# Two transformer blocks with grouped experts: slot table loaded by ScalarE, rows of the first expert stage gathered by one-hot products, and another hand-over between the blocks

## The reference, cut to what matters

```python
def hier_moe(x2d, w_grp, b_grp, w_exp, b_exp, w_gate, w_up, w_down):
    ...                       # combine[t, e]: two weights per token
    for e in range(N_EXPERTS):
        h = jax.nn.silu(x2d @ w_gate[e]) * (x2d @ w_up[e])
        y = y + combine[:, e:e + 1] * (h @ w_down[e])
    return y
# first_block:  h = h + mix @ w_out;  h = h + moe(rmsnorm(h, norm_ffn_g));  return rmsnorm(h, final_norm_g)
# second_block: the same with rms_norm, starting from the first block's output x:
#   u = rms_norm(x, attn_norm) @ w_in;  h = x + mix @ w_out_2;  h = h + moe(rms_norm(h, ffn_norm_2)); return rms_norm(h, final_norm_2)
```

## Time and profile before

| | us |
|---|---|
| median of 3 runs | 1642.69 (1637.81 to 1642.77) |
| profiled execution, its own time | 1649.94 |
| its span | 1648.2 |
| around the span | 1.7 |
| PE busy | 1389.2 (84%) |
| DVE busy | 428.0 (26%) |
| ACT busy | 363.0 (22%) |
| POOL busy | 188.7 (11%) |
| mean granted TensorE clock | 0.919 |
| DMA traffic | 287.90 MB |

### The profile page before, as it was taken

The page is one execution under the profiler, slowest core; times in us unless marked ns, Lnnn a source line. Parts: engine busy times, 40 slices in busy tenths (PEclk is TensorE's granted clock), DMA queues, the critical chain, the costliest instruction groups (busy, mean ns, idle before and its releaser), DMA issues. The chain is left out here.

```text
span 1648.2 us, 22613 instructions
## 1 busy us (share of the span) xinstructions
PE 1389.2 (84%) x9850; PEld 696.6 (42%) x9850; DVE 428.0 (26%) x797; ACT 363.0 (22%) x617; POOL 188.7 (11%) x259
## 2 busy tenths in 40 slices
PE   5999989877897688876679999568789799999995
PEld 3434444577555233322334444367445533333332
DVE  2233315432324001101520100493522400000015
ACT  2023016443122011111231100332433111111112
POOL 5000002254001110110000000141000110000000
PEclk8989999999998798999879999886899799999998
DMA  5251100200144699999613210000224479998973
GB/s 192 97 215 51 51 0 0 104 4 4 57 179 179 241 410 417 416 414 411 228 51 124 80 52 0 1 1 1 103 76 160 176 290 365 350 344 338 347 324 132
DMA packets 77418, 287.90 MB, mean 175 GB/s; under 512 B 17057, under 2 KB 18424, under 8 KB 65026
## 3 DMA queue, kind: packets, MB, share of 16 engines
q1 hardware_dynamic: 67456, 265.33, 41.7%
q0 software_dynamic: 7680, 14.72, 2.6%
q10 hardware_dynamic: 2178, 6.34, 1.0%
HBM read 267.50 MB, written 29.84 MB: 180 GB/s over the span
## 5 line engine op out<-in xcount | busy, mean ns | idle before, releaser
L347 PE MATMUL banks<-mixT,ring 128*128 128x512 f32 x672 | 295.4, 602 | 0.8 <-DVE mixT L2400 0.8
L347 PEld LDWEIGHTS banks<-mixT,ring 128*128 128x128 f32 x672 | 130.2, 194 | 165.6 <-issue 164.4
L2144 PE MATMUL banks<-arena_moe,mixT 128*32 128x512 f32 x768 | 174.6, 601 | 0.0
L2144 PE MATMUL banks<-ring,mixT 128*32 128x512 f32 x768 | 118.0, 621 | 18.8 <-DMA arena_moe<-in_w_up 15.5
L1446 PE MATMUL banks<-ring,mixT 128*128 128x512 f32 x256 | 116.0, 609 | 8.2 <-PEq L51 8.2
L1891 PE MATMUL banks<-arena_moe,mixT 128*64 128x512 f32 x256 | 69.5, 703 | 34.1 <-DMA arena_moe<-in_exp_w_up 34.1
L344 PE MATMUL banks<-ring,mixT 128*128 128x512 f32 x192 | 82.9, 593 | 0.0
L2144 PEld LDWEIGHTS banks<-ring,mixT 128*32 128x32 f32 x768 | 37.9, 114 | 95.9 <-issue 95.9
L1446 PEld LDWEIGHTS banks<-ring,mixT 128*128 128x128 f32 x256 | 48.9, 196 | 65.6 <-issue 65.6
L1891 PE MATMUL banks<-ring,mixT 128*64 128x512 f32 x256 | 60.0, 623 | 10.9 <-DMA ring<-in_exp_w_up 7.7
L1740 DVE TENSOR_TENSOR mixT<-banks,params 128x512 f32<-128x512 f32 (+1 forms) x64 | 38.8, 623 | 111.6 <-PE banks L1731 100.6
(11 more groups left out here) (421 smaller groups left out, 1996.4 us busy)
## 6 DMA issues: line engine op xcount, KB each, us to landing
ring<-in_w_in SPq DMA_DIRECT2D x18, 1024.0 KB, 8.4
arena_moe<-in_exp_w_gate SPq DMA_DIRECT2D x16, 1024.0 KB, 13.0
arena_moe<-in_exp_w_up SPq DMA_DIRECT2D x16, 1024.0 KB, 17.9
arena_moe<-in_exp_w_down SPq DMA_DIRECT2D x16, 1024.0 KB, 22.7
ring<-in_exp_w_gate SPq DMA_DIRECT2D x16, 1024.0 KB, 14.3
ring<-in_exp_w_up SPq DMA_DIRECT2D x16, 1024.0 KB, 18.9
ring<-in_exp_w_down SPq DMA_DIRECT2D x16, 1024.0 KB, 22.4
arena_moe<-in_w_gate SPq DMA_DIRECT2D x8, 2048.0 KB, 11.0
```

The costliest lines, as they stand in the source:

```text
L347: last = pe.matmul(bank[:], w[:, c, i * P:(i + 1) * P], m.mixT[:, c, :], start=(c == 0), stop=(c == DC - 1))
L2144: last = pe.matmul(hb[u][T * i:T * (i + 1), :], z.xe[:, j, at:at + T], both[:, :, j, half * 256:half * 256 + 256], start=(j == 0), stop=(j ...
```

## The change

It does the following.

1. `load_slots` for the main table moves from SP to ScalarE's program in both blocks: after silu 1 of body 0, before hidden_taken 0. ScalarE no longer waits for the slots before body 0, but before output 0 of body 0.
2. Block 1: all bodies get their rows by one-hot products. VectorE writes G for body i+2 behind the rows of body i+1; TensorE runs 2 x 32 matmuls in place of 2 x 8 transposes; the 14 fetches by GpSimd go. Block 2: body 1 alone gets its rows that way; bodies 2 to 7 fetch as before, the fetch for body 2 being issued first.
3. `between_programs`: the scaling `store` and its write by ScalarE go; SP writes the gained rows (hg) to HBM, between the second and the third weight item of the projection. Block 2's residual is scaled when it is added (`scalar_tensor_tensor` with a kept factor in place of `tensor_tensor`). `taken(0)` to `taken(2)` move in between the statistics of later tiles, and the second square writes to another scratch.
4. Last body of block 1: early(0) and early(1) come before the `y_low_dve`, early(2) and early(3) after them.
5. Start: the two norm gains of the expert blocks are no longer loaded as rows by ScalarE and turned, but loaded turned by SP, element by element (2 x 1024 elements of 4 bytes), behind the small loads.

```diff
@@ load_slots: sp.dma_start becomes engine.dma_start; out_programs: add(i, n)
-            dve.tensor_tensor(h, h, m.banks[k % 3][:], ALU.add)
+                dve.scalar_tensor_tensor(h, h, residual_scale(i), m.banks[k % 3][:], ALU.mult, ALU.add)
@@ phase_project1, sync
+            for name, c in TURNED.items():
+                sp.dma_start(m.params[:, c:c + DC], io[name].rearrange("l (c p) -> p (l c)", p=P),
+                             allow_slow_non_contiguous=True).then_inc(ph.sem("turned_gains"), 16)
@@ gather_pe(pe, ph, z, pair, half, taken): 32 matmuls per half
+    for a in range(2):
+        if taken is not None:
+            pe.wait_ge(ph.sem("gathered_taken"), taken + a + 1)
+        for b in range(2):
+            j = 4 * half + 2 * a + b
             for t in range(NT):
                 for part in (z.x_hi, z.x_lo):
...
@@ narrow_programs, sync
-        sp.wait_ge(out.sem("tabled"), TABLED)
-        z.load_slots(sp, z.main, 0, ph.sem("slots"))
@@ narrow_programs, gpsimd
-        fetch_rows(pool, ph, z, z.main.fetch[:, 1, :])
...
-            if i + 2 < NB:
-                pool.wait_ge(ph.sem("gathered"), 4 * (i + 1) + 4)
-                fetch_rows(pool, ph, z, z.main.fetch[:, i + 2, :])
@@ narrow_programs, tensor, body
-                turn_rows_pe(pe, ph, m, z, gath, 0, 32 * (i + 1), None)
+                pe.wait_ge(ph.sem("onehot"), ONEHOTS * (i + 2))
+                gather_pe(pe, ph, z, gath, 0, None)
...
-                turn_rows_pe(pe, ph, m, z, gath, 1, None, 4 * (i + 1))
+                gather_pe(pe, ph, z, gath, 1, 4 * (i + 1))
@@ narrow_programs, vector
+        onehot_dve(dve, ph, m, z, 1)
...
+            if i + 2 < NB:
+                onehot_dve(dve, ph, m, z, i + 2)
...
+        early(0)
+        early(1)
         for c in range(2):
             for n in range(2):
                 y_low_dve(...)
-        for t in range(NT):
-            early(t)
+        early(2)
+        early(3)
@@ narrow_programs, scalar (wide_programs alike, with output 0 waiting for the slots)
-        act.wait_ge(ph.sem("slots"), 64)
+        def load_slots():
+            act.wait_ge(out.sem("tabled"), TABLED)
+            z.load_slots(act, z.main, 0, ph.sem("slots"))
...
-            hiddens(ph, i)
+            hiddens(ph, i, None if i else load_slots)
             if i:
                 act.wait_ge(ph.sem("placed"), 32 * i)
+            else:
+                act.wait_ge(ph.sem("slots"), SLOTS_LOADED)
@@ wide_programs, tensor: body 1's rows
+            if n == 1:
+                pe.wait_ge(ph.sem("onehot"), 2 * ONEHOTS)
+                gather_pe(pe, ph, z, gath, half, taken)
+            else:
+                turn_rows_pe(pe, ph, m, z, gath, half, 32 * (n - 1), taken)
@@ between_programs
+        def keep():
+            for t in range(NT):
+                sp.wait_ge(ph.sem("gained"), t + 1)
+                sp.dma_start(rows[:, t, :], hg[:, t, :]).then_inc(ph.sem("stored"), 16)
...
-            act.activation(store[:, t, :], hg[:, t, :], ACT.Copy, scale=stat(t, I1)).then_inc(ph.sem("unscaled"), 1)
-            act.wait_ge(ph.sem("unscaled"), t + 1)
-            act.dma_start(rows[:, t, :], store[:, t, :]).then_inc(ph.sem("stored"), 16)
...
+            v.mark(dve.tensor_copy(kept_scale(m, t), stat(t, I1)))
...
+        dve.wait_ge(ph.sem("squares"), 2 * NT - 2)
+        taken(0)
         means(NT - 1)
         inverses(NT - 2)
+        taken(1)
         inverses(NT - 1)
-        dve.wait_ge(ph.sem("squares"), 2 * NT)
-        for t in range(NT):
-            taken(t)
+        taken(2)
+        taken(3)
```

More of the change, by code:

```diff
@@ L1705, in place_rows, with gather_pe @@
                                 oob_is_err=False).then_inc(ph.sem("placed"), 16)
[L1708 to L1712, removed]
+def gather_pe(pe, ph, z, pair, half, taken):
+    for a in range(2):
[3 more added lines that the diff above has]
+            j = 4 * half + 2 * a + b
             for t in range(NT):
                 for part in (z.x_hi, z.x_lo):
-                    last = pe.matmul(banks[b][:, at:at + z.slots], part[:, t, j * P:(j + 1) * P], z.G[:, t, :],
+                    last = pe.matmul(pair[a][:, b * z.slots:(b + 1) * z.slots], part[:, t, j * P:(j + 1) * P], z.G[:, t, :],
                                      start=(t == 0 and part is z.x_hi), stop=(t == NT - 1 and part is z.x_lo))
@@ L1844, in begin @@
             sp.wait_ge(x.sem("body_done"), r * NB + 1)
+            sp.wait_ge(out.sem("tabled"), TABLED)
             z.load_slots(sp, z.extra, (r + 1) * cap, x.sem("slots"))
@@ L2039, in further_pool, with first_rows_pe, further_pe @@
     further.run(pool, lambda r: None, body, lambda n: pool.nop())
-def first_rows_pe(pe, ph, out, z, banks, onehots):
+SLOTS_LOADED = 64
+def first_rows_pe(pe, ph, out, z, first, second):
     pe.wait_ge(out.sem("split"), NT)
-    pe.wait_ge(ph.sem("onehot"), onehots)
-    gather_pe(pe, ph, z, banks)
-def further_pe(pe, further, z, x, x_ring, banks, body):
+    pe.wait_ge(ph.sem("onehot"), ONEHOTS)
+    gather_pe(pe, ph, z, first, 0, None)
+    gather_pe(pe, ph, z, second, 1, None)
+def further_pe(pe, further, z, ph, x, x_ring, first, second, body):
     def end(n):
@@ L2053, in end @@
         pe.wait_ge(x.sem("body_done"), done + 1)
-        gather_pe(pe, x, z, banks)
+        gather_pe(pe, x, z, first, 0, None)
+        gather_pe(pe, x, z, second, 1, None)
         for s in range(z.EB):
@@ L2060, in further_pe, with further_dve @@
     further.run(pe, lambda r: None, body, end)
-def further_dve(dve, further, m, z, x, banks, gain, rest):
+def further_dve(dve, further, m, z, x, first, second, gain, rest):
     def begin(r):
-        dve.wait_ge(x.sem("slots"), 64 * r + 64)
+        dve.wait_ge(x.sem("slots"), SLOTS_LOADED * r + SLOTS_LOADED)
         slots_known(dve, z, z.extra, x.sem("known"), KNOWN * r)
@@ L2078, in end @@
         for half in range(2):
-            turned_rows_dve(dve, x, m, z, banks[2 * half:2 * half + 2], gain, n * z.bodies, half)
+            turned_rows_dve(dve, x, m, z, second if half else first, gain, n * z.bodies, half)
     further.run(dve, begin, body, end)
@@ L2286, in scalar @@
             silu(ph, i, 1)
+            if i == 0:
+                act.wait_ge(out.sem("tabled"), TABLED)
+                z.load_slots(act, z.main, 0, ph.sem("slots"))
             hidden_taken(ph, i, 0)
@@ L2329, in final_programs, with kept_scale @@
     return sync, None, scalar, vector
+def kept_scale(m, t):
+    return m.small[:, 20 + t:21 + t]
 def between_programs(m, io, z, ph, experts, dst, y):
     rows = dst.rearrange("b (t p) d -> p (b t) d", p=P)
-    hg, store, scaled = z.outs[0], z.outs[1], z.h
+    hg, spare, scaled = z.outs[0], z.outs[1], z.h
+    spare2 = z.ring23[:, 1, 0:NT * D].rearrange("p (t d) -> p t d", d=D)
     p_sync, p_tensor, p_scalar, p_vector = project2_programs(m, io, ph, y)
```

91 lines of the change are left out of this document (52 added, 39 removed).

## The result

The changed kernel takes 1632.33 us (median of 10 runs, 1627.68 to 1636.49) against 1642.73 us in the same set (10 runs, 1636.67 to 1645.52). The ratio is 0.994, 95% interval 0.9927 to 0.9954: 10.4 us faster, where 2.2 were forecast. The two profiled executions are 20.2 us apart (1649.94 and 1629.70 us). Two bodies of block 2 in the profile of before took 40.2 and 40.5 us by SP's rows, where its others took 37.8 to 37.9. The changed kernel's trace has none like that.

A forecast was written before the change was run, and what follows sets the result against it. Weights' DMA was taken to bound block 1's expert loop, PE's chain and the load behind it block 2. Terms -5.8 - 8.9 + 6 - 3.7 - 3.2 + 13.4 = -2.2 from 1642.7 gave 1640.5 us, range 1619 to 1650.

The forecast's parts named there:

- the forecast's own case: Whole kernel: slots land late behind weights and stall both blocks; 1640.5 us, spanning 1634 to 1648, chance 0.58.
- Start of block 1's loop: Block 1: with slot loads gone from SP, the expert loop's transfers start at 544.9; -5.8 us.
- Fetched rows: Block 1's loop: 3.67 MB of fetches on q0 go, at 414 GB/s; -8.9 us, bounds 0 to twice that.
- Gathers at 0 in block 1: Block 1: gathers lengthen a PE body to 29.1 us, still covered by 31.6 us of transfers; 0.
- Slot loads in block 1: Block 1, body 0: slots land at about 584, output 0 waits, later loads go late; +6 us, bounds 0 and 12.
- rival 2: Both blocks: ScalarE is also held issuing slot loads because a queue takes limited packets ahead; 1650 us, chance 0.15.
- the issues overlapped well before: Slot-load issue, both blocks: the prediction's argument that ScalarE would not be held while issuing; no size of its own.
- Slot loads in block 2: Block 2, body 0: slots land at 1361.7, delaying output 0 and body 1; +13.4 us, bounds 0 and 18.
- Rival 1: Both blocks: slots land early, elements bundled or let through between large packets, so neither block stalls; 1624 us, chance 0.27.
- Last body: End of block 1: two tiles' additions move into VectorE's wait for the last outputs; -3.7 us.
- hand-over: Between the blocks: ScalarE's chain loses its `store` steps, VectorE's `taken` takes back about 1.4; -3.2 us.
- Turned gains: Start of the kernel: 2048 tiny packets on q1 are covered by SP's idle time before the third weight item; 0.

The follow-up runs named there:

- e8: The kernel before, unchanged, profiled once more; 1648.2 us for one run.
- e10: Changed kernel with block 1's four slot loads issued by SP again, ahead of body 1's weights; block 2 stays with ScalarE; 1631.02 us, ratio 0.9927.
- e4: Changed kernel with block 1's rows of bodies 2 to 7 fetched by GpSimd and transposed again, body 1 still gathered; 1649.37 us, ratio 1.0034.
- e1: Changed kernel with block 2's four slot loads issued by SP again, ahead of body 1's weights; block 1 stays with ScalarE; 1625.43 us, ratio 0.9877.
- e6: Changed kernel with all eight additions of block 1's last body behind the four low parts again; 1643.38 us, ratio 0.999.
- e2: Changed kernel with ScalarE's slot loads moved ahead of silu 0 in both blocks; 1620.10 us, ratio 0.9857.
- e7: Changed kernel with ScalarE's fourth slot load moved behind hidden_taken 1 (block 1) and hidden_taken 2 (block 2), the first three left in place; 1624.18 us, ratio 0.9862.
- e3: Changed kernel with the slot loads issued by GpSimd in both blocks as soon as its own scatter has landed; 1620.39 us, ratio 0.985.
- e5: Changed kernel with the hand-over of before: two ScalarE scalings per tile, its write to HBM, unscaled residual, turned tiles taken at the end; 1641.78 us, ratio 0.9985.
- e11: Changed kernel with the two expert-block norm gains loaded as rows by ScalarE and turned again, SP's single elements gone; 1634.87 us, ratio 0.995.

## Why the prediction was right in its range and wrong in its sum

The time lies inside the range of 1619 to 1650 and on the side given 0.45. The sum was 8 us too slow, and 1632.3 lies outside the 1634 to 1648 that the forecast's own case was given. That the sum came this near is partly luck: its two largest terms for the slot loads have about the right size for a wrong reason.

- **Start of block 1's loop, -5.8.** Right in kind: -5.2 between the two profiles. But e8's profile of before gives 3.1 us and e10, with block 1's slot loads on SP again, 2.2. The saving depends on how late the scattered table lands: the slot loads were issued at 545.45, after the first `gate_up` had ended, at 543.71 in e8 and 541.27 in e10, before it had.
- **Fetched rows, -8.9.** This term failed in size. The bytes of q0 over the stretch of the loop fell by 3.61 MB (7.34 to 3.73), 8.7 us, as forecast. But q1's bytes by the time of the last `gate_up` fell too, 87.61 to 85.52 MB, 5.0 us more. Of these 2.09 MB, 0.52 are the final gain, which SP now loads before the stretch; the rest is down weights of body 7, moved while a late DMA engine still held up the last `gate_up`'s load. Together that is 13.7 us, inside the bounds of 0 to 17.8. e4 shows the same pair from the other side, +3.04 and +1.51 MB, and 12.3 us in all for six of seven fetches. I had counted what a fetch moves, not that it leaves the DMA engines uneven. The full clock of the last `gate_up` (8.60 to 7.09 us) came on top, but e1 and e6 show that the changed kernel does not always get it.
- **Gathers at 0 in block 1.** Right: a body takes the 29.1 us forecast (29.3), and e4 excludes that the gathers cost what they save. TensorE did set the pace of some bodies (575 to 663), while the queue worked ahead.
- **Slot loads in block 1, +6.** Size near, mechanism wrong, and so luck. The step that failed is "the issues overlapped well before", the argument against rival 2. The issue was held for 12.74 us, TensorE for 9.37, and e2 prices it at 7.6 us. No output waited for slots: the hold itself kept the down weights back and emptied q1, so that they landed at 567 and not at 584. Where the issue was not held (e7), they landed at 587.6 and TensorE waited 10.37 us, where 5 or so were forecast.
- **Slot loads in block 2, +13.4.** Again rival 2's mechanism at, by luck, the forecast's size: 10 to 12 us for the hold (e1) and 1.6 for the gathers. The forecast saw the slots landing 30 us behind their issue and holding output 0; that is what e7 shows (36 us), not the changed kernel (25 us). Equal turns were right, but I let a later queue of 2048 packets wait in the queue, where only about 1,580 fit. Rival 2's own +16 was too high, because the issue ends when the last load fits, not when the backlog is through.
- **Rival 1, slots early.** The Trainium skill, page "DMA: Bandwidth & Descriptors", section "Queues, rings and completion order", has a DMA engine go round its queues by packet, with typically some 9 to 17 descriptors in one. The trace agrees with the first half (119 to 119). On ScalarE's queue each element was a packet, 4224 for 4096 elements with their completions, so the second half does not hold there. On GpSimd's queue the same elements were bundled, 256 packets in all (e3). Since the elements took their turns one by one, the slots did not land early behind weights.
- **Last body -3.7, hand-over -3.2.** Both right: 3.2 (the first profile of before) to 4.9 us (e6, e8) and 4.0 us (e5) by the traces.
- **Turned gains, 0.** Missed: 1.1 to 1.3 us won at the start (e11). I had looked only at what the new loads might cost, not at the two that leave the path.

With the measured terms: -5.2 - 8.7 - 5.0 - 1.5 (clock) + 7.6 - 4.9 - 4.0 + 12 - 1.2 = -10.9, against -10.4 by the medians. The terms are not known as well as that agreement looks: the start is 2.2 to 5.2, block 1's hold 3 to 7.6, the last body 3.2 to 4.9, and block 2's stall 11.7 to 13.9.

The held issue could have been read from the trace of before. There SP stands in the same way behind its own backlog, which I did not look for because nobody waits for it. Two of its rows in block 1:

```profile
730.58 0.89 SPq L1380 DMA_DIRECT2D ring<-in_exp_w_down  x2
735.40 6.01 SPq L1380 DMA_DIRECT2D arena_moe<-in_exp_w_down  x2
```
Two loads of the same size each time: 0.89 us with room in the queue and 6.01 without. An SP that is held costs nothing until its next load is due; ScalarE stood in TensorE's chain.

## What to carry to other kernels

Moving a load to another engine moves its issue as well. Before giving a load of many small elements to an engine on the path, look in the trace for issues that lasted longer than their like, and put it where the other queues are empty, even if its data is needed much later (e2), or on an engine whose issue nobody waits for (e3). Freeing the issue alone is not enough if the data then comes late (e7). In a stage bound by transfers, a removed transfer can be worth more than its bytes: look whether all DMA engines are still busy when the last load that counts lands.

## What the hardware showed that I had not expected

- The hold is sudden: in block 2 three issues behind weights take 1.6 us (e7), the fourth 17 us (the changed kernel). What the hold costs and what late data costs are two things: in the changed kernel no output waits for slots, in e7 they wait 27.90 and 16.80 us.
- GpSimd's queue bundles 8-byte elements that ScalarE's queue sends one by one: 256 packets against 4224. Its issue of four loads is as short (2.86 us) as SP's or ScalarE's on empty queues (2.69 to 3.43).
- With fetches beside the weights the DMA engines finish unevenly: for 4 us at the end of block 1 they move only 28 to 30 GB/s, about what one engine does, and the last loads land only then (before, e4). Without fetches 376 GB/s still move at the same distance from the last `gate_up` where it was 135 and 142.
- Packets take turns one to one at any ratio of sizes seen, 8 bytes against 16 KB (119 to 119 in 4 us), and q1 kept 99.2% of the engines' time while 16 KB of slots needed over 20 us.
